# Sixteen gate products moved out of the gate stage into the block inversion, and the box pooling from the pool engine to the vector engine

## What is computed

```python
def box_mean_grid(u, window, rows):
    ...
    s = corner(r1, c1) - corner(r0, c1) - corner(r1, c0) + corner(r0, c0)
    cnt = ((r1 - r0)[:, None] * (c1 - c0)[None, :]).astype(jnp.float32)[None, :, :, None]
    return (s / cnt).reshape(B, T, C).astype(u.dtype) - u

def pool_branch(u, mean_fn, w_pool, pool_scale, w_b_out):
    outs = [jnp.einsum('btc,cd->btd', mean_fn(u[..., j * POOL_GROUP:(j + 1) * POOL_GROUP], win), w_pool[j])
            for j, win in enumerate(POOL_WINDOWS)]
    return (jnp.concatenate(outs, axis=-1) * pool_scale) @ w_b_out

def merge_branches(z, ya, mean_fn, b_gate, w_pool, pool_scale, w_b_out, w_o):
    yb = pool_branch(z[..., SHIFT_COLS:SHIFT_COLS + D_B], mean_fn, w_pool, pool_scale, w_b_out)
    gates = jax.nn.sigmoid(z[..., SHIFT_COLS + D_B:] + b_gate)
    m = gates[..., :D_MODEL] * ya + gates[..., D_MODEL:] * yb
    return m @ w_o
```

## Time and profile before

| | us |
|---|---|
| time of the kernel, median of 3 runs | 2649.95 |
| lowest and highest of them | 2646.48, 2656.65 |
| the profiled execution, its time | 2655.38 |
| its span, first to last instruction | 2653.7 |
| `gates`, 396 to 548 of the span | 152 |
| `invert`, 548 to about 755 | 207 |

### The profile page before, as it was taken

The page is one execution under the profiler, slowest core; times in us unless marked ns, Lnnn a source line. Parts: engine busy times, 40 slices in busy tenths (PEclk is TensorE's granted clock), DMA queues, the critical chain, the costliest instruction groups (busy, mean ns, idle before and its releaser), DMA issues.

```text
span 2653.7 us, 41107 instructions
## 1 busy us (share of the span) xinstructions
PE 2117.1 (80%) x16489; PEld 1345.7 (51%) x16489; DVE 1670.8 (63%) x3486; ACT 849.1 (32%) x1661; POOL 737.5 (28%) x607
## 2 busy tenths in 40 slices
PE   5899959974468998978789987777777778777876
PEld 2777737763468888856545543233333333332332
DVE  2589983338702444355477777777777777777764
ACT  4466642334432333332332322221222212222121
POOL 0000009100011212100234444544444444444441
PEclk9899989975568899889899999998898989999999
DMA  4467754250144333153699999999999999999995
GB/s 175 146 205 251 245 200 162 83 215 1 49 180 158 111 134 137 36 177 110 267 420 417 408 393 415 415 420 420 421 420 420 421 420 420 420 420 421 421 420 209
DMA packets 131280, 742.05 MB, mean 280 GB/s; under 512 B 17392, under 2 KB 24592, under 8 KB 64528
## 3 DMA queue, kind: packets, MB, share of 16 engines
q0 software_dynamic: 73728, 536.90, 48.8%
q1 hardware_dynamic: 56208, 200.41, 20.8%
q10 hardware_dynamic: 1152, 2.10, 0.2%
HBM read 683.67 MB, written 55.69 MB: 279 GB/s over the span
## 4 chain that ended last, share of the span: by engine, by line
DMA 30%; PE 13%; DVE 4%; issue 3%; ACT 2%; POOL 1%; POOLq 0%; DVEq 0%; ACTq 0%
DMA uvx<-in_uv_in,ic 27%; PE bank L2371 10%; DVE junk L2260 2%; DMA uv<-in_uv_in,ic 1%; POOL uvx L2097 1%; DMA scores_dram<-later 1%; PE bank L91 1%; PE bank L93 1%; PE bank L92 1%; ACT dg L2174 0%; PE bank L2352 0%; DVE wql L2226 0%; ACT ge L2169 0%; ACT L2169 0%; POOL uv L2097 0%
## 5 line engine op out<-in xcount | busy, mean ns | idle before, releaser
L2371 PE MATMUL bank<-uv,dg 128*128 128x512 f32 x1664 | 816.2, 648 | 208.5 <-ACT dg L2174 208.4
L2371 PEld LDWEIGHTS bank<-uv,dg 128*128 128x128 f32 x1664 | 335.3, 206 | 679.0 <-issue 404.6
L2097 POOL DMA_INDIRECT uv<-in_uv_in,ic x416 | 481.7, 1158 | 624.3 <-PE bank L2371 550.5
L2260 DVE SCALAR_TENSOR_TENSOR junk<-uv,gr 128x1024 f32<-128x1024 f32 x416 | 509.7, 1225 | 187.2 <-DMA uv<-in_uv_in,ic 157.7
L2169 ACT ACTIVATE ge<-dt_ 128x4 f32<-128x4 f32 x128 | 26.3, 205 | 946.5 <-DVE junk L2260 946.4
L2371 PE MATMUL bank<-uvx,dg 128*128 128x512 f32 x384 | 187.8, 646 | 57.5 <-ACT dg L2174 57.5
L2174 ACT ACTIVATE dg<-ident,gc_ 128x128 f32<-128x128 f32 x512 | 163.7, 390 | 29.4 <-DVE gc_ L2266 29.4
L91 PE MATMUL bank<-ht_hi,wh 128*128 128x256 f32 (+1 forms) x432 | 152.2, 352 | 22.9 <-DVE wl L587 22.9
L2371 PEld LDWEIGHTS bank<-uvx,dg 128*128 128x128 f32 x384 | 77.0, 206 | 168.2 <-issue 90.9
L2260 DVE SCALAR_TENSOR_TENSOR junk<-uvx,gr 128x1024 f32<-128x1024 f32 x96 | 117.7, 1226 | 59.9 <-DMA uvx<-in_uv_in,ic 57.1
L2097 POOL DMA_INDIRECT uvx<-in_uv_in,ic x96 | 112.6, 1173 | 124.0 <-PE bank L2371 114.2
(11 more groups left out here) (333 smaller groups left out, 3825.0 us busy)
## 6 DMA issues: line engine op xcount, KB each, us to landing
pair_record<-rec SPq DMA_DIRECT2D x40, 768.0 KB, 4.2
wt<-in_wrow_in SPq DMA_DIRECT2D x32, 512.0 KB, 4.5
wraw<-in_wpair_in SPq DMA_DIRECT2D x24, 512.0 KB, 3.6
ab<-pair_record SPq DMA_DIRECT2D x16, 768.0 KB, 6.0
wz<-in_wz_in SPq DMA_DIRECT2D x20, 512.0 KB, 3.3
wm<-in_wmod SPq DMA_DIRECT2D x4, 2048.0 KB, 21.0
wraw<-in_wq_in SPq DMA_DIRECT2D x16, 512.0 KB, 7.4
uv<-in_uv_in,ic POOLq DMA_INDIRECT x416, 28.1
```

What stands on the lines that cost most here:

```text
L2097: pool.indirect_dma_start(ring(i), None, g["uv_in"], bass.IndirectOffsetOnAxis(ap=ic[:, s % ICR, k:k + 1], axis=0)).then_inc(su[row_slot[i ...
L2260: dve.scalar_tensor_tensor(junk[:, :], ring(i)[:, 0:D], 1.0, hc[:, t % 2, :], ALU.mult, ALU.mult, accum_out=dt[:, k:k + 1]).then_inc(s_ud, 1)
L2371: mm = pe.matmul(acc(t, c)[:, :], dg[:, n % 2, k, :], ring(i)[:, D + 512 * c:D + 512 * c + 512], start=h == 0 and q == 0 and k == 0, stop= ...
```

## The change

The stage `gates` becomes `pools` and keeps the four pooling inputs, the pooling and the eight output tiles, which are now stored ungated in the new `yb_dram`. The box adds are DVE instructions, the widest window first, with a grid `cr` of its own for the row sums, so that nothing has to be zeroed in between; POOL only zeroes at the start. PE takes the output tiles of the first four column blocks by quarters, as each window's result comes.

The sixteen gate tiles become 32 half tiles (four of the eight k steps, 12 matmuls) in `invert`: `gate(m)`, m = 0 to 31. To keep the tokens there, they are held as `hx_hi` and `hx_lo` through `invert`; the context tokens lie apart and are given up before. `front` therefore writes high and low parts in two pieces. The gates take PSUM banks 3 and 7, so the other steps rotate two or three banks. ACT makes the high part of half tile m + 2 after gate(m), and for each whole tile a tanh, for gate a also the scaling. DVE makes the low parts (`low(m)`) and the gated product, in the chain of the inversion after every second step u; `low(m)` waits for gate(m - 2) to have been multiplied. SP loads the half tiles, three buffers deep, in between the other loads and stores.

```diff
-def gates(nc, sb, sem, g):
+def pools(nc, sb, sem, g):
...
+    ORDER = tuple(reversed(range(NW)))
...
+                for i in range(NW - 1):
+                    low(i)
+                pooled(0)
+                low(NW - 1)
+                for j in range(4):
+                    out_low(j)
+                for i in range(1, NW):
+                    pooled(i)
+                    pooled_low(i - 1)
+                pooled_low(NW - 1)
+                for j in range(4, NPAIR):
+                    out_low(j)
...
+                for i in range(NW):
+                    pool_product(i)
+                    if i:
+                        pe.wait_ge(s_plo, i)
+                        for j in range(4):
+                            yb(j, i - 1)
                 pe.wait_ge(s_plo, NW)
...
+                for j in range(4):
+                    yb(j, NW - 1).then_inc(s_yb, 1)
+                for j in range(4, NPAIR):
+                    for i in range(NW):
+                        mm = yb(j, i)
                     mm.then_inc(s_yb, 1)
...
+                for m in range(9, NZ):
+                    weights(m)
+                    if m % 4 == 1:
+                        gated((m - 9) // 4)
+                    if m % 4 == 3:
+                        branch((m - 11) // 4 + 2)
+                    if m == 28:
+                        stored(0)
...
+                def high(m):
+                    if m >= NZ:
+                        return
+                    act.wait_ge(s_wz[m % 3], 16 * (m // 3) + 16)
+                    if m >= 2:
+                        act.wait_ge(s_gp, m - 1)
+                    act.activation(wzh[:, m % 2, :, :], wz[:, m % 3, :, :], ACT.Copy).then_inc(s_gh, 1)
...
+                def low(m):
+                    dve.wait_ge(s_gh, m + 1)
+                    if m >= 2:
+                        dve.wait_ge(s_gp, m - 1)
+                    dve.tensor_tensor(wzl[:, m % 2, :, :], wz[:, m % 3, :, :], wzh[:, m % 2, :, :].bitcast(FP32),
+                                      ALU.subtract).then_inc(s_gl, 1)
...
                         ch(dve.tensor_tensor(gz[:, :, 0:n, n:HB], gz[:, :, 0:n, n:HB], o, ALU.add))
+                        if u % 2 and m0 < (17, NZ)[b]:
+                            low(m0)
+                            if m0 % 4 == 3:
+                                gated((m0 - 7) // 4)
+                            m0 += 1
...
+                def gate(m):
+                    t, h = divmod(m, 2)
+                    pe.wait_ge(s_gl, m + 1)
+                    if h == 0 and t >= 2:
+                        pe.wait_ge(s_gk, t - 1)
+                    for k in range(KH):
+                        K = h * KH + k
+                        mm = split_mm(pe, bank[ZB[t % 2]][:, :], wzh[:, m % 2, k, :], wzl[:, m % 2, k, :], hx_hi[:, K, :], hx_lo[:, K, :],
+                                      K == 0, K == KT - 1)
+                    mm.then_inc(s_gp, 1)
...
+                for i in range(NG):
+                    products(0, i)
+                    gate(i)
+                for n in range(16):
+                    turned_in(0, n)
+                for i in range(NG):
+                    products(1, i)
+                    gate(4 + 2 * i)
+                    gate(5 + 2 * i)
+                for n in range(16):
+                    turned_in(1, n)
+                    if n % 4 == 3:
+                        gate(12 + n // 4)
+                gate(16)
                 turned_out(0)
-                combined(0)
+                gate(17)
+                gate(18)
+                for r in range(6):
+                    inner(0, r)
+                    if r % 2:
+                        gate(19 + r // 2)
+                for r in range(6):
+                    corner(0, r)
+                    if r % 2:
+                        gate(22 + r // 2)
+                for m in range(25, NZ):
+                    gate(m)
                 turned_out(1)
-                combined(1)
+                for r in range(6):
+                    inner(1, r)
+                for r in range(6):
+                    corner(1, r)
```

More of the change, by code:

```diff
@@ L1231, in _ @@
[L1231 to L1236 removed]
+                    if r >= 3:
+                        pe.wait_ge(s_yc, 12 * b + 2 * (r - 2))
+                    for u in range(16):
+                        for p in range(2):
+                            mm = pe.matmul(bank[r % 3][quarter(p, 1), HB * u:HB * u + HB], tu[quarter(p, 0), 16 * r + u, HB:CHUNK],
+                                           xy[quarter(p, 0), 16 * r + u, :], start=True, stop=True)
```

622 lines of the change are left out of this document (344 added, 278 removed).

## The result

The changed kernel took 2602.41 us (median) against 2646.48 us for the kernel before, a ratio of 0.983 with a 95% interval of 0.981 to 0.986: faster by 44 us. One of its five executions took 9875.39 us, at a granted clock of 0.187; the interval leaves it out, and the median of the other four is 2598.7. The forecast was 2616, 34 us faster, with a range of 2597 to 2643; the rival (a), the clock better than thought, said 2598, and the measured time lies nearer to it.

The account below looks back on a forecast made before the run. PE was taken to bound `gates`, DVE the inversions; -82 + 13 + 23 + 9 + 2 + 1 = -34 us took the profiled 2655.4 to 2621, or 2616 us against the median 2650, range 2597 to 2643.

Parts of the forecast that it names:

- rival (a): In `invert`, PE is never late and half products lift the small products' clock; only DVE's instructions count: 2598 us, chance 0.20.
- `pools`, -82: Sixteen z products leave the stage and pooling stands bare on DVE; it ends at 463.2 in place of 545.1 us.
- the far bound: Box adds in `pools` at POOL's own rate, 2.9 ns per element, instead of DVE's 1.035 ns.
- rival (c): Pooling adds in `pools` cost twice the price taken, 24 us more: 2640 us, chance 0.05.
- First inversion, +13: Thirteen `low` and three gated products on DVE, 11.0 us, plus 2 for waits; bounds +11 and +40.
- Hand-over and second inversion, +23: DVE instructions 13.1 us, wait at `low(19)` 3.9, clock changes 6; 67.3 becomes 90.3 us, bounds +13 and +49.
- clock changes in the groups: Second inversion: 6 us allowed for PE's clock changing in the twelve groups of 32x32 products.
- three banks for four: Turns out and 32x32 products in `invert`: fewer banks cost nothing, since ACT's copies pace them.
- Opening, +9: Start of `invert`: four half products +7.3 to +16.9, turns on two banks up to 4, less up to 6.8; bounds 0, +21.
- up to 6.8: Opening of `invert`: four groups of small products may give back this many us by running at full clock.
- (b): Rival: half the half products in `invert` at half clock, some 21 us above the forecast: 2637 us, chance 0.17.
- (d): Rival: all 32 half products at 1.2 GHz, PE bounds `invert`; +31, slower than before at 2681 us, chance 0.06.

Follow-up runs that it names:

- e4: Changed kernel with each low part of the gate weights and each gated product in `invert` cut to 16 of 512 elements: 2588.1 us, 0.980 of the kernel before.
- e5: Changed kernel with six more 128x512 matmuls, results thrown away, ahead of each even half product in `invert`: 2611.1 us, 0.986 of the kernel before.
- e2: Changed kernel with the 20 box adds of `pools` left out: 2596.0 us, 0.982 of the kernel before.
- e6: Changed kernel with bank 7 as fourth bank in the turn out, and `low(19)` one step later: 2604.1 us, 0.982 of the kernel before.
- e3: Changed kernel without the 32 half products in `invert`, their loads, splits, tanh and gated products; banks as changed: 2574.3 us, 0.972 of the kernel before.
- e10: Changed kernel run again with no edit: 2601.5 us, 0.982 of the kernel before.
- e9: Changed kernel with all 32 `low` of `invert` on POOL, gated products still on DVE: 2604.9 us, 0.983 of the kernel before.

## Why the prediction was right, and where it was not

**The bound and the direction** were right: a stage that PE bounds gave up 87 us of matmuls, and DVE, which bounds the inversions, got instructions for them. e4 and e5 show both halves of that: 0.5 us less for each DVE instruction came out of the first inversion in full and out of the second stretch but for 1.5 us, and of 22 us more of PE the first inversion showed nothing and the second stretch 3. The table by stage has every sign as predicted.

**`pools`, -82 against -84.3.** The DVE chain came out as worked through, box adds included; the far bound, POOL's rate, and rival (c) fall with the first window's rows, 0.69 us for 512 elements. `invert` began at 465.0, predicted 466. Two sizes are off. Up to window 16 the recorded terms (7.6, 0.6, 1.05 and 1.2 us after 401.6) add up to 412.1 and not to 412.9; measured from the first product it began after 10.5 us, which is their sum. And the 2.4 us for twelve matmuls at 1.2 GHz were put among the output products. Twelve did run so, but in the fourth z product; what they cost is part of the 1.85 us that DVE waits ahead of the first `p_lo`, where the prediction had 0.5, and from 444.10 us on PE runs its last 72 matmuls 0.23 us apart. `wb` ahead of the third weight tile cost at most the 0.38 us that ACT waited for that tile. What the prediction didn't see is how narrowly this chain leads: e2 shows that PE's z products and the hops to ACT lie only 8 us behind it.

**First inversion, +13 against +9.7.** The term that was mis-sized is the price of an instruction: 0.69 us was taken, from a duration, for an instruction whose successor starts 0.61 us later. 16 x 0.61 = 9.8 is the whole of it; the 2 us for waits were not there.

**Hand-over and second inversion, +23 against +15.4.** Three terms. The 19 DVE instructions: 11.6 in place of 13.1. The wait at `low(19)`: 2.75 in place of 3.9; the mechanism was right, and e4 and e6 show that its date hangs on ACT and PE, not on DVE's step; of gate 17's twelve matmuls five ran at 1.2 GHz, where the prediction had all. The 6 us for "clock changes in the groups" did not exist, which is the largest miss of the sum: between 593 and 631 us, where the groups stand, the granted clock was 0.99, and DVE waits nowhere behind `low(19)`. Against that stands what I put at nothing, three banks for four: +1.1 in the trace of after, and e6 with a fourth gets 1.3 back.

**Opening, +9 against +6.1; tail, +2 against +1.7; `front`, +1 against +1.1.** In the opening, e3 divides the growth into 2.6 for the half products and 3.5 that stay without them; the turns on two banks, 12.56 against 9.75 us, are 2.8 of these, inside the "up to 4". The half products thus cost 2.6 us of the 10.9 that they take on PE at full clock: the rest lies in waits for loads (not divided up here), and in three groups of small products at 2.50 to 2.86 us in place of 4.3, which is some 5 of the "up to 6.8". In the tail the trace has what the prediction named: the turn out waits for gate 31 and begins 1.7 us after the end of the second inversion. To the tenth the agreement is worth little, since kernels with the same `invert` have tails of 52.2 to 53.6 us.

**The clock.** The prediction took the earlier trace rows, where 32x32 products alone stay at 1.2 GHz, as a sign that half products in bursts would begin at 1.2 GHz, and gave this 0.17 (b) and 0.06 (d). The trace says otherwise. PE's rows in the second inversion where a half product begins, and the clock by short stretches, columns as in the earlier trace rows:

```profile
630.77 0.50 PE L91 MATMUL bank<-hx_hi,wzh 128*128 128x512 f32 x1 [1.77 <-DVE wzl L1263]
636.18 0.50 PE L91 MATMUL bank<-hx_hi,wzh 128*128 128x512 f32 x1 [0.81 <-DVE wzl L1263]
641.30 0.73 PE L91 MATMUL bank<-hx_hi,wzh 128*128 128x512 f32 x1 [2.05 <-DVE wzl L1263]
```

```profile
576.00:593.00 17.00, 12.55 (x65) 10.21 (x64) 10.19 (x14) 16.62 (x24) 0.00 (x0) 0.52 0.06 19
593.00:631.00 38.00, 36.23 (x862) 29.69 (x862) 34.36 (x37) 22.74 (x38) 0.00 (x0) 0.99 0.28 91
631.00:635.00 4.00, 4.00 (x12) 3.08 (x11) 3.90 (x4) 0.00 (x0) 0.00 (x0) 0.57 0.78 290
...
641.00:645.00 4.00, 3.70 (x9) 2.94 (x10) 3.90 (x6) 0.00 (x0) 0.00 (x0) 0.57 0.70 235
```

For 38 us PE stays at 2.4 GHz while half products and 32x32 groups alternate, the same 32x32 products that were at 1.2 GHz in the earlier trace rows. It falls back at the hand-over, where PE has mostly turns, and for single groups behind waits of 1.77 and 2.05 us. DVE feels the first, through gate 17 and `low(19)` (0.66 us between two executions of the same kernel, e10), and neither of the others: after 597.48 it has no wait of over 0.15 us. The length of the wait alone does not decide: behind the same 1.77 us, the same group of e10 (631.53 us) ran at full clock throughout. So rival (a) was the better description of the clock. The Trainium skill's page "TensorE: Matmul & The Clock Gate", section "HAM oscillation — how this bites in real kernels", speaks of short groups of matmuls with waits between them that begin throttled each time. The trace agrees for the groups behind the longest waits (424.16, 631, 641) and not for those behind shorter ones, as at 636.18, and there the measurement decides.

**The total.** The sum missed by 16 us at the start of `scan` (-50 for -34): 2.3 in `pools`, 2.9 in the opening, 3.3 in the first inversion, 7.6 in the second stretch, 0.3 in the tail. All of these lie on one side: most unknowns were given a price above zero, and most of those had none. Of the 16, `scan`'s scatter hid 4 in the pair of profiles, so part of the agreement is luck: the profiled pair misses by 13.5, the medians by 10. Rival (a), with 2598, comes closer, and in part by luck too: its -82 + 30 = -52 meets the measured -50, but it has nothing for the opening, which cost 6.1, and prices DVE's instructions at 0.69.

## What to carry to other kernels

Work moved into a stage that another engine bounds costs what it adds to that engine's stream, start to start, and not the duration in a row: read the distance of two starts where nothing waits in between. An idle POOL is no free helper for a DVE that is the bound; each subtraction moved to it cost DVE's chain 0.99 us in the first inversion (estimated from e3 and e9), against 0.61 if DVE does it. And when a change takes banks from steps that rotated over four, price each of these steps: here 64 turns on two banks for four took 2.8 us more, and a fourth bank beside three was worth 1.3.
